# Residual kept in the buffer of the expert sums, gate applied by GpSimd before the scatter, one row a token loaded at the end

## What is computed

```python
x = x + gate1 * y
h2 = rmsnorm(x) * (1 + scale2) + shift2
x = x + gate2 * moe_ffn(h2)
out = rmsnorm(x)
```

## Time and profile before

| | us |
|---|---|
| median of 3 runs | 3126.94 (3125.61 to 3128.7) |
| the profiled execution | 3128.19 |
| its span, first to last instruction | 3126.6 |
| TensorE busy | 2696.8 (86%) |
| VectorE busy | 1854.2 (59%) |
| ScalarE busy | 1519.5 (49%) |
| GpSimd busy | 319.9 (10%) |

### The profile page before, as it was taken

One profiled execution on the slowest core, in us unless ns is written; L12 is line 12 of the kernel. 1 busy time (PEld: TensorE's weight loads), 2 busy tenths in 40 slices (PEclk: granted clock), 3 DMA queues, 4 the chain that ended last, 5 costly groups with the idle time before them and its releaser, 6 DMA issues. The chain is left out here.

```text
span 3126.6 us, 42533 instructions
## 1 busy us (share of the span) xinstructions
PE 2696.8 (86%) x12590; PEld 2152.3 (69%) x12591; DVE 1854.2 (59%) x2645; ACT 1519.5 (49%) x2204; POOL 319.9 (10%) x369
## 2 busy tenths in 40 slices
PE   1499979896797825999999999999999999999994
PEld 0388857674586624787787777877887777777771
DVE  6611034443553344866767686688666868866865
ACT  1222124343342105755556675587555757765751
POOL 0000011010000032101111110111111101110100
PEclk8699989996898857999999999999999999999995
DMA  8422132211333245966868697699676988967966
GB/s 340 177 101 75 51 97 85 65 58 37 102 114 130 89 156 173 329 210 217 299 214 280 226 350 242 190 350 339 206 231 222 347 261 288 328 227 251 322 215 210
DMA packets 424898, 641.07 MB, mean 205 GB/s; under 512 B 28960, under 2 KB 345008, under 8 KB 421504
## 3 DMA queue, kind: packets, MB, share of 16 engines
q1 hardware_dynamic: 394656, 558.79, 52.1%
q0 software_dynamic: 27872, 73.01, 8.8%
q10 hardware_dynamic: 2304, 8.39, 0.7%
HBM read 595.88 MB, written 64.73 MB: 211 GB/s over the span
## 5 line engine op out<-in xcount | busy, mean ns | idle before, releaser
L2104 DVE TENSOR_TENSOR e_gu_lo<-gu_raw,e_gu_hi 128x1024 fp32r<-128x1024 f32 x564 | 680.3, 1219 | 176.4 <-ACT e_gu_hi L1980 171.5
L82 PE MATMUL e_pgu<-e_gu_hi,e_x_hi 128*128 128x512 f32 x1568 | 643.0, 410 | 5.5 <-issue 5.5
L1980 ACT ACTIVATE e_gu_hi<-gu_raw 128x1024 fp32r<-128x1024 f32 x564 | 576.6, 1050 | 104.2 <-SPq L1789 81.5
L84 PE MATMUL e_pgu<-e_gu_hi,e_x_lo 128*128 128x512 f32 x1568 | 614.7, 392 | 0.0
L83 PE MATMUL e_pgu<-e_gu_lo,e_x_hi 128*128 128x512 f32 x1568 | 612.9, 391 | 0.0
L84 PEld LDWEIGHTS e_pgu<-e_gu_hi,e_x_lo 128*128 128x128 f32 x1568 | 294.5, 188 | 65.1
L2110 DVE TENSOR_TENSOR e_dn_lo<-dn_raw,e_dn_hi 128x1024 fp32r<-128x1024 f32 x280 | 332.9, 1218 | 9.7 <-ACT e_dn_hi L1986 9.6
L82 PE MATMUL e_pdn<-e_dn_hi,e_a_hi 128*128 128x512 f32 x784 | 310.0, 395 | 24.4 <-DVE e_a_lo L2138 23.5
L82 PEld LDWEIGHTS e_pgu<-e_gu_hi,e_x_hi 128*128 128x128 f32 x1568 | 295.2, 188 | 51.1 <-issue 5.9
L83 PEld LDWEIGHTS e_pgu<-e_gu_lo,e_x_hi 128*128 128x128 f32 x1568 | 296.6, 189 | 46.5
L84 PE MATMUL e_pdn<-e_dn_hi,e_a_lo 128*128 128x512 f32 x784 | 306.5, 391 | 0.0
(11 more groups left out here) (356 smaller groups left out, 4079.7 us busy)
## 6 DMA issues: line engine op xcount, KB each, us to landing
gu_raw<-in_w_gate_up_dram SPq DMA_DIRECT2D x572, 512.0 KB, 8.8
dn_raw<-in_w_down_dram SPq DMA_DIRECT2D x142, 1024.0 KB, 10.3
wada<-in_w_ada_dram SPq DMA_DIRECT2D x24, 1024.0 KB
win_raw<-in_w_in_dram POOLq DMA_DIRECT2D x6, 2048.0 KB
gu_bias<-hidden_bias SPq DMA_DIRECT2D x42, 256.0 KB, 9.9
proj_by_token<-out_stage SPq DMA_DIRECT2D x32, 256.0 KB, 2.0
wg_raw<-in_w_in_dram POOLq DMA_DIRECT2D x16, 512.0 KB, 4.9
gates_transposed<-g_stage POOLq DMA_DIRECT2D x32, 256.0 KB, 2.3
```

The costliest lines, as they stand in the source:

```text
L82: pe.matmul(out, a[0], w[0], start=first, stop=False)
L84: return pe.matmul(out, a[1], w[0], start=False, stop=last)
L1980: act.activation(gu_hi[:, b, 2 * j:2 * j + 2], gu_raw[:, b, 2 * j:2 * j + 2].rearrange("p k g n -> p k (g n)"), ACT.Copy).then_inc(gu_hi_d ...
L2104: dve.tensor_tensor(gu_lo[:, b, 2 * j:2 * j + 2], gu_raw[:, b, 2 * j:2 * j + 2].rearrange("p k g n -> p k (g n)"), gu_hi[:, b, 2 * j:2 * j ...
```

## The change

The residual is stored into the rows of the buffer that the scatters add to; only the padding rows are still zeroed. GpSimd multiplies each evacuated block by `gate2` in place, before the scatter, with a semaphore of its own between the two. The last stage loads one row a token, multiplies only the bias part by `gate2`, and adds the row.

```diff
@@ phase_out, sync
-                sp.dma_start(m.x2[rows, :], x2[:, t % 2]).then_inc(stored[t % 2], 16)
+                sp.dma_start(m.y_sum[rows, :], x2[:, t % 2]).then_inc(stored[t % 2], 16)
@@ phase_route, sync
-            for t in range(NT + 1):
-                sp.dma_start(m.y_sum[t * P:(t + 1) * P, :], zero[:]).then_inc(zero_out, 16)
+            sp.dma_start(m.y_sum[SEQ:SEQ + P, :], zero[:]).then_inc(zero_out, 16)
...
-            sp.wait_ge(zero_out, 16 * (NT + 1))
+            sp.wait_ge(zero_out, 16)
@@ phase_experts, gpsimd
             def scatter(s, blocks):
 
                 wait_apart(pool, y_out, blocks + 2)
+                pool.tensor_tensor(ys[:], ys[:], m.gate2[:], ALU.mult).then_inc(gated, 1)
+                wait_apart(pool, gated, blocks + 2)
                 pool.indirect_dma_start(out=m.y_sum[:, :], out_offset=bass.IndirectOffsetOnAxis(ap=dest[:, 0, s, 0:1].bitcast(U32), axis=0),
                                         in_=ys[:], in_offset=None, compute_op=ALU.add).then_inc(scattered, 16)
 
+            pool.sem_inc(gated, 2)
@@ phase_combine, sync
                 sp.dma_start(y[:, b], m.y_sum[t * P:(t + 1) * P, :]).then_inc(y_in[b], 16)
-                sp.dma_start(x2[:, b], m.x2[t * P:(t + 1) * P, :]).then_inc(y_in[b], 16)
@@ phase_combine, tensor
-                    pe.wait_ge(summed, t - 1)
+                    pe.wait_ge(gated, t - 1)
@@ phase_combine, vector
-                dve.wait_ge(y_in[b], 32 * (t // 2 + 1))
                 dve.wait_ge(biased, t + 1)
                 if t >= 2:
 
                     dve.wait_ge(done, t - 1)
-                dve.tensor_tensor(acc[:, b], y[:, b], ps[:, b], ALU.add).then_inc(summed, 1)
-                dve.wait_ge(summed, t + 1)
-                dve.tensor_tensor(acc[:, b], acc[:, b], m.gate2[:], ALU.mult).then_inc(gated, 1)
+                dve.tensor_tensor(acc[:, b], ps[:, b], m.gate2[:], ALU.mult).then_inc(gated, 1)
+                dve.wait_ge(y_in[b], 16 * (t // 2 + 1))
                 dve.wait_ge(gated, t + 1)
-                dve.tensor_tensor(acc[:, b], acc[:, b], x2[:, b], ALU.add).then_inc(x3, 1)
+                dve.tensor_tensor(acc[:, b], acc[:, b], y[:, b], ALU.add).then_inc(x3, 1)
```

More of the change, by code:

```diff
@@ L1733, in phase_experts @@
         y_out = sem("e_y_out")
+        gated = sem("e_gated")
         scattered = sem("e_scattered")
@@ L2206, in phase_combine @@
         y = sb(ctx, "c_y", [P, 2, D], F32)
-        x2 = sb(ctx, "c_x2", [P, 2, D], F32)
         bd = sb(ctx, "c_bd", [NE, D], F32)
@@ L2217, in phase_combine @@
         biased = sem("c_biased")
-        summed = sem("c_summed")
         gated = sem("c_gated")
@@ L2311, in build @@
         m.lrT = dram("low_rank_transposed", [RANK, SEQ])
-        m.x2 = dram("residual", [SEQ, D])
         m.h2 = dram("ffn_input", [SEQ, D])
@@ L2315, in build @@
         m.hidden_bias = dram("hidden_bias", [NE, 2 * FF])
-        m.y_sum = dram("expert_sum", [SEQ + P, D])
+        m.y_sum = dram("residual_sum", [SEQ + P, D])
         PASSED[:] = [nc.alloc_semaphore("passed")]
```

## The result

The changed kernel takes 3149.84 us (median of 4 runs, 3147.0 to 3152.09) beside 3127.82 us for the kernel before on the same chip (3125.61 to 3132.18): a ratio of 1.0071, 95% interval 1.0055 to 1.0087. It is 22.0 us slower; the prediction was 3152. The profiled execution took 3151.53 us.

What follows compares the result with a forecast made beforehand. TensorE, busy 2696.8 of 3126.6 us, was taken as the bound, held by VectorE in the expert stage. Terms 22.0 + 7.8 + 4.9 - 9.3 = +25.4 us gave a forecast of 3152 us, 8-in-10 range 3124 to 3175.

Steps and rivals of the forecast that it cites:

- Price of a multiply: Expert stage, GpSimd: one multiply of 1024 elements a partition takes 2.3 us, between 1.04 and 2.8 us.
- M: The time of one GpSimd multiply in the expert stage, taken as 2.3 us.
- the 128-element row times eight: Estimate of one multiply from GpSimd's 292 ns affine select of 128 elements a partition: 2.34 us.
- VectorE is held too: Expert stage: while GpSimd multiplies, a VectorE subtract with two SBUF inputs waits; subtract 2.01 us late in one-block rounds.
- Single rounds: Rounds with one block: multiply makes e_act 1.10 us late for TensorE, 20 times, 22.0 us.
- First slots ahead of a double round: First block's multiply, next round with two blocks, 14 times: e_act about 1.0 us late, costing nothing.
- The cover of 1.7 us: Before a two-block round: e_act done near 1420.7, TensorE takes it at 1422.42, which hides the delay.
- Second slots: End of two-block rounds, 13 times: e_a_lo 0.5 us later, net 0.6 us each, 7.8 us.
- The later landing of this scatter: End of two-block rounds: scatter 2.5 us later costs nothing; 5 us if the cover were gone.
- The 1.5 us in hand: Two-block round behind another, 5 times: slack of ACT's evacuation against the scatter's landing, called the tightest case.
- Last round: End of the expert stage: two multiplies in series and about 0.1 us to start each, 4.9 us.
- Last stage: Final tile-by-tile VectorE chain: one operation a tile goes, period 5.27 to 4.02 us, 9.3 us gained.

Runs made afterwards that it cites:

- no_multiply: Changed kernel without GpSimd's multiply by gate2 and the wait behind it; 3117.32 us, ratio 0.9964 to the kernel before.
- memset_instead: Changed kernel with four GpSimd memsets of an unused buffer in place of the multiply; 3136.39 us, ratio 1.0025 to the kernel before.
- copies_instead: Changed kernel with two GpSimd copies of e_y onto itself in place of the multiply; 3160.62 us, ratio 1.0107 to the kernel before.
- split_multiply: Changed kernel with the multiply in two 512-channel halves, the second in one-block rounds timed for VectorE's idle time; 3154.87 us, ratio 1.0095 to the kernel before.

## Why the prediction was right

Right by its mechanism. The total is as close as it is partly by luck: two terms were wrong the opposite way (-3.9 us and +2.5 us). By its own steps, predicted and measured by the table:

- *Price of a multiply, 2.3 us.* Measured 2.38 us alone, 2.72 when it first waits for VectorE. The Trainium skill (GPSIMD Engine Reference, section 3.1) gave an estimate of 2.25 us; the trace has 6% more. (By the prediction's own slopes, 35 us of time for 1 us of M, its sum would be 1.8 us lower with it, not 2 to 3.) That 2.3 came out is luck in part: "the 128-element row times eight" multiplies the fixed part too. With 1.28 us for 512 elements and 2.38 for 1024 the multiply has about 0.18 us fixed and 2.15 ns an element, between two and three of the passes that the prediction counted.
- *VectorE is held too.* Shown: subtracts of 3.02 and 3.44 us beside multiplies, none in no_multiply or memset_instead. The Trainium skill (SBUF — State Buffer, "Who interferes with whom") says that a VectorE operation with two SBUF inputs contends with a GpSimd one that reads SBUF, and not with one that only writes; by copies and memsets the traces agree (subtracts of 1.64 us beside copies, 1.22 beside memsets).
- *Single rounds, 22.0 us.* Measured 20.4; it is the change's main cost. The 12 rounds behind single ones lose 0.93 us each where 1.1 was predicted, since the subtract ended 1.80 us late instead of 2.01. The 8 behind double ones lose 1.16 us on average, which the prediction did not tell apart: 1.9 us more together. Late weights fit these (ACT's wait for them is 34.9 us instead of 10.0), but no run takes them apart.
- *First slots ahead of a double round, 0.* Right: 0.1 us besides the late landings, though a subtract is held in each of these rounds (2.1 to 2.7 us instead of 1.22). The cover of 1.7 us hides it.
- *Second slots, 7.8 us.* Measured 3.9 (0.24 to 0.39 each). The step that failed is "`e_a_lo` comes 0.5 us later ... Net 0.5 to 0.7 us": the race was won by GpSimd, as I let it be, but TensorE's wait moved forward to the piece itself (0.54 us) and took the place of its wait for `e_a_lo`; the two don't add.
- *"The later landing of this scatter costs nothing by my sum."* Wrong: ACT waited 0.3 to 0.9 us in the five double rounds behind double ones, and TensorE lost 2.5 us there. I had priced it at 5 us if the cover were gone; half of that came. The 1.5 us in hand were not the tightest case, as I had called them: in the trace before the five rounds have 1.5, 1.8, 0.7, 0.7 and 1.7 us, because the landing itself varies. Against them stood a shift of 2.58 us (+3.41 instead of +0.83).
- *Last round, 4.9.* Measured 4.8.
- *Last stage, -9.3.* Measured -9.4, with 4.05 us a tile. The terms written down for it (10.0 + 0.6 - 0.9) make 9.7; the rest was put down to rounding.

These make 23.4 us between the traces, with 1.1 us ahead of the first block that no step names, against 25.4; between the medians it is 22.0 us.

What stays open: why the landing takes from 9.2 to 11.3 us behind the start of the scatter in those five rounds. It is longest in copies_instead (10.9 to 11.3), but not in step with the start: split_multiply starts it later still and has 10.3 to 11.0, and the kernel before has 9.5 to 10.6. Open too is which part of the loss in single rounds behind double ones is late weights.

## What to carry to other kernels

An idle engine isn't free to use when its reads of SBUF hold up the engine that the critical one waits for. Here 2.4 us of a GpSimd that is busy for only 14% of the time cost 0.9 us of TensorE in each single round behind a single one, until they were cut and placed into VectorE's own idle stretches. Cost such an operation by how far it sticks out of that idle time (halving it took nearly nine tenths of the cost away). Before placing it, also follow the buffer it works on: a scatter that started 2.6 us later was a stall where the next writer had 0.7 to 1.8 us in hand. Cutting an operation in two where the other engine is waiting lets that engine in between, and the pair comes out longer than the whole.

## What the runs showed of the hardware that I had not expected

- When a multiply on GpSimd starts 0.03 to 0.04 us ahead of a two-input subtract of VectorE (14 times in the changed kernel), VectorE's record holds the wait: 3.44 us for 1.22 us of work. Such a hold isn't in any list of waits; it shows only as a longer instruction.
- GpSimd's one-input copies and VectorE's subtracts hold each other as wholly as the multiply does, and memsets of the same partitions not at all. The one that is held ends its own length, less 0.12 to 0.14 us, behind the end of the other, in both directions. A held subtract ends 1.07 to 1.09 us behind the multiply or copy nearly everywhere (48 of 48 times in the changed kernel; its own length is 1.22). A held copy ends 0.90 us behind the subtract (its own 1.04), a held multiply 2.27 us (its own 2.39).
- A scatter starts 0.83 us behind the end of the multiply, copy or memset that it waits for on its own engine (two or three of the 49 start 1.74 us behind). The same 0.83 us stood behind ACT's evacuation before. So an added operation delays the scatter by its own length and the 0.2 us that it takes to start.
